# Hybrid decoder step: four scoring steps for eight, the own token through TensorE, copies of the value product on ScalarE

## What is computed

```python
gate = jnp.einsum('bshd,bnhd->bhsn', q, k_mean)        # one number per head and block
_, idx = lax.top_k(gate, ks)                           # the 3 best blocks
s_sel = jnp.einsum('bqhd,bhqnjd->bhqnj', q_c, k_sel) - slopes * dist
s_own = jnp.einsum('bqhd,bjhd->bhqj', q_c, k_own)      # for a sample: its own new token
p = jax.nn.softmax(concat(s_sel, s_own))
o = einsum(p_sel, v_sel) + einsum(p_own, v_own)
```

## Time and profile before

| | |
|---|---|
| median of 3 runs | 666.08 us (663.58 to 670.77) |
| the profiled execution | 667.34 us, its span 665.6 us |
| PE, DVE, ACT, POOL busy | 566.9, 420.4, 240.2, 135.4 us |
| mean granted TensorE clock | 0.922 |
| the eight turns | 121.45 us to 360.42 us |

### The profile page before, as it was taken

How to read it: one execution, slowest core, us unless ns; L and a number is a source line. 1 busy time by engine, 2 the same in 40 slices (tenths; PEclk the granted TensorE clock), 3 DMA queues, 4 the chain that set the end, 5 groups by cost and what they waited for, 6 DMA issues and landing times.

```text
span 665.6 us, 10279 instructions
## 1 busy us (share of the span) xinstructions
PE 566.9 (85%) x4080; PEld 463.0 (70%) x4080; DVE 420.4 (63%) x735; ACT 240.2 (36%) x438; POOL 135.4 (20%) x206
## 2 busy tenths in 40 slices
PE   4869998778778797868679597977999999999997
PEld 2657686546455554536446586966999999999997
DVE  2425793598797979887865366346655666664441
ACT  1102311454462727342135143136433344333341
POOL 8110100274746657661010000000000000000000
PEclk9969998798888887979988899976999999999999
DMA  8998297439896887898472739644775845466600
GB/s 264 384 413 311 73 406 245 160 127 387 285 401 254 348 330 279 342 373 349 162 296 85 261 130 391 225 133 148 232 254 191 286 158 182 120 173 175 176 34 33
DMA packets 85199, 159.30 MB, mean 239 GB/s; under 512 B 2572, under 2 KB 61112, under 8 KB 81047
## 3 DMA queue, kind: packets, MB, share of 16 engines
q1 hardware_dynamic: 79328, 89.27, 40.4%
q0 software_dynamic: 5120, 67.71, 25.7%
q10 hardware_dynamic: 703, 1.67, 0.7%
HBM read 156.39 MB, written 2.72 MB: 239 GB/s over the span
## 4 chain that ended last, share of the span: by engine, by line
PE 61%; DVE 15%; DMA 13%; POOL 4%; ACT 3%; issue 3%; ACTq 1%; SPq 1%; POOLq 0%; DVEq 0%
PE acc L1200 13%; PE acc L1291 12%; PE acc L1292 11%; PE acc L1293 11%; DMA kring<-in_cache_k,rowof 5%; PE chain L1376 4%; DVE prod L819 3%; DVE sall L826 3%; POOL cvT L471 3%; PE acc L1167 3%; DMA wring<-in_w_ada 2%; DMA wring<-in_w_out 2%; DMA wring<-in_w_attn_proj 1%; DMA wring<-in_w_ffn_in 1%; DVE wlo L896 1%
## 5 line engine op out<-in xcount | busy, mean ns | idle before, releaser
L1200 PE MATMUL acc<-hT,wring 128*128 128x264 f32 x576 | 158.8, 430 | 3.7 <-DVE hT L785 1.9
L896 DVE TENSOR_TENSOR wlo<-wring,whi 128x1024 fp32r<-128x1024 f32 (+2 forms) x92 | 101.9, 1108 | 93.2 <-ACT whi L499 92.5
L1200 PEld LDWEIGHTS acc<-hT,wring 128*128 128x128 f32 x576 | 116.5, 210 | 36.7 <-issue 13.5
L1291 PE MATMUL acc<-xlo,whi 128*128 128x264 f32 x416 | 123.9, 298 | 13.5 <-DVE xT L1070 7.4
L499 ACT ACTIVATE whi<-wring 128x1024 fp32r<-128x1024 f32 (+2 forms) x92 | 88.2, 963 | 119.4 <-PE acc L1293 94.3
L1292 PE MATMUL acc<-xhi,wlo 128*128 128x264 f32 x416 | 120.9, 291 | 0.0
L1293 PE MATMUL acc<-xhi,whi 128*128 128x264 f32 x416 | 120.9, 291 | 0.0
L471 POOL TENSOR_TENSOR cvT<-cvT,cprod 128x256 f32<-128x256 f32 x120 | 88.2, 735 | 86.6 <-ACT cprod L499 71.3
L1291 PEld LDWEIGHTS acc<-xlo,whi 128*128 128x128 f32 x416 | 81.2, 195 | 18.2 <-DVE wlo L896 8.6
L819 DVE TENSOR_TENSOR prod<-kring,qbc 128x1024 f32<-128x1024 f32 x64 | 77.4, 1210 | 7.5 <-DMA kring<-in_cache_k,rowof 3.3
L1292 PEld LDWEIGHTS acc<-xhi,wlo 128*128 128x128 f32 x416 | 81.7, 197 | 0.1
(11 more groups left out here) (221 smaller groups left out, 623.5 us busy)
## 6 DMA issues: line engine op xcount, KB each, us to landing
wring<-in_w_ada SPq DMA_DIRECT2D x24, 1024.0 KB, 8.2
wring<-in_w_ffn_in SPq DMA_DIRECT2D x22, 1024.0 KB, 6.8
wring<-in_w_in SPq DMA_DIRECT2D x12, 1024.0 KB, 19.1
wring<-in_w_ffn_out SPq DMA_DIRECT2D x16, 704.0 KB, 5.8
wring<-in_w_out SPq DMA_DIRECT2D x4, 1024.0 KB
wring<-in_w_in SPq DMA_DIRECT2D x6, 512.0 KB, 14.3
wring<-in_w_in SPq DMA_DIRECT2D x4, 768.0 KB, 12.2
wring<-in_w_conv_proj SPq DMA_DIRECT2D x2, 1024.0 KB, 15.7
```

Of the source, the lines that this page charges most:

```text
L896: v.tensor_tensor(wlo[:, place, 0:n, :], w, whi[:, place, 0:n, :].bitcast(F32), ALU.subtract)\
L1200: ins = mm(bank[:, 0:R], w[:, k, P * t:P * t + P], src[:, k, :], start=k == 0, stop=k == KD - 1)
L1291: mm(bank[:, 0:R], whi[:, place, k - k0, :], lo[:, k, :], start=k == 0, stop=False)
```

## The change

- **Four scoring steps**: STEPS is 4, each pair works on 2048 elements a partition. The first multiply of the next sample stands at the turn's start, ahead of the copy of the page sums; the others are moved too.
- **K in three places**: a chunk of K goes in turn to the two halves of `kring` and to place 2 of the weight ring, which the turns' weights give up (they use places 0 and 1). The ring of tap products has four places.
- **PSUM**: the small products of the chain go to a bank of their own, `small`; `chain` holds only the value product, `psO` shares the bank of `psT`. The next L1313 doesn't wait for the last reads of the turn.
- **Own token**: its V row of each sample lies in partitions 32 to 39 (`vrow`), DVE makes an 8 x 8 of probabilities that is zero but for row b (`pown`), and PE adds one more matmul of 8 rows into column group 0 of the value product. DVE's L1016 and L1037 go.
- **Value product**: probabilities `pg` of 8 columns, unpadded; the sums are copied out by ACT; the mask `headof` goes into the sums over partitions, which PE does behind the next prompt scores; ACT copies their result into `oT`.
- **Prompt**: ACT scales the rows of the prompt's probabilities, behind its second batch of tap products; the product with V stands behind the spread of the sums.
- **Ranking of blocks**: one subtraction and two fused operations for four.
- ACT does the convolution's silu (now `conv_rows`) before it copies the last value product.

The core of the diff:

```diff
-STEPS = 8
+STEPS = 4
...
+K_RING = 3
...
+PLACE = dict(zip(SLOTS, [0, 1, 2, 0, 1, 2, 0, 1] + [n % 2 for n in range(B - 1)]))
...
-CONV_RING = 5
+CONV_RING = 4
...
+        psO = psT
...
+        k_place = [kring[:, 0:PC, :], kring[:, PC:PG, :], wring[:, 2, :].rearrange("p (j n) -> p j n", j=PC)]
```

On POOL (gathers), and on ACT in a turn:

```diff
             for b in range(B):
                 add_taps(b, 0)
                 add_taps(b, 1)
-                if b + 2 < B:
-                    gather_k(b + 2, 0)
+                gather_k(CH * b + 5)
                 add_taps(b, 2)
...
-                if b + 2 < B:
-                    gather_k(b + 2, 1)
+                gather_k(CH * b + 6)
...
+                tap_products(b, 1)
+                act.wait_ge(prin_ready, b + 1)
+                for t, (c0, c1) in enumerate(((0, P), (P, 384))):
+                    func(pr[:, c0:c1], pr[:, c0:c1], ACT.Copy, scale=prin[:, t:t + 1]).then_inc(pn_ready, 1)
                 act.wait_ge(pt_ready, b + 1)
                 act.wait_ge(pp_ready, b)
                 func(prT[:, :], psT[:, 0:384], ACT.Copy).then_inc(pc_ready, 1)
-                tap_products(b, 1)
...
+                if b == B - 1:
+                    conv_rows()
+                act.wait_ge(v_used, CH * (b + 1))
+                func(pvm[:, :], pv[:, :], ACT.Copy).then_inc(pvm_ready, 1)
+                if b < B - 1:
+                    gate(FIRST_GATE[b] + 1)
+                act.wait_ge(pv_ready, b + 1)
+                for e in range(2):
+                    rows = slice(DH * e, DH * e + DH)
+                    func(oT[rows, :, S + b], pvT[rows, e:H:2], ACT.Copy).then_inc(o_ready, 1)
```

On PE, the own token and the end of a turn:

```diff
-                        ins = mm(chain[32 * q:32 * q + 32, :], ppad[:, g, :], vring[:, g, :],
-                                 start=g < 4, stop=g >= PG - 4)
+                        ins = mm(pv[32 * q:32 * q + H, :], pg[:, g, :], vring[:, g, :], start=g < 4, stop=PG - 4 < g)
+                        if g == PG - 4:
+                            mm(pv[0:H, :], pown, vrow, start=False, stop=True)
...
-                pe.wait_ge(pvm_ready, b + 1)
-                for t in range(AT):
-                    ins = mm(chain[:, t:t + 1], pvm[:, P * t:P * t + P], ones[:, 0:1], start=True, stop=True)
-                ins.then_inc(pv_ready, 1)
-
                 if b + 1 < B:
                     if b == B - 2:
                         pe.wait_ge(ln_c, 2)
                         sums("lnv", lnsq, CT)
                     prompt_scores(b + 1)
+
+                pe.wait_ge(pvm_ready, b + 1)
+                for t in range(AT):
+                    ins = mm(pvT[:, 2 * t:2 * t + 2], pvm[:, P * t:P * t + P], headof[:, 2 * t:2 * t + 2], start=True, stop=True)
+                ins.then_inc(pv_ready, 1)
                 if b in THIRD:
                     tile(THIRD[b], mix, 2, hT, k1=4)
```

More of the change, by code:

```diff
@@ L476, in _ @@
             pool.wait_ge(w_full[0], 64)
[L477 to L479 removed]
+            gather_k(0)
+            gather_k(1)
+            pool.wait_ge(acc_full, NUMBER[LAST_FILL["k"]] + 1)
+            gather_k(2)
             for c in range(CH):
                 gather_v(0, c)
[L482 removed]
+            gather_k(3)
+            gather_k(4)
             for b in range(B):
@@ L832, in score @@
                 add_up(b, half)
-            for half in range(4):
+            for half in range(STEPS // 2):
                 score(0, half)
@@ L1032, in _ @@
                     dve.wait_ge(stored, 16 * 7)
-                dve.wait_ge(pv_ready, b + 1)
-                dve.wait_ge(dve_step, at_own)
-                for e in range(2):
-                    rows = slice(DH * e, DH * e + DH)
-                    v.tensor_tensor(oT[rows, :, S + b], own[rows, :], chain[rows, 0:AT], ALU.add).then_inc(o_ready, 1)
-                add_up_next(7)
             for t in range(1, KD):
@@ L1263, in _ @@
             to_rows("vn1", vT, P, P)
-            to_rows("vs", vT, S, B)
+            bank = bank_for("vs")
+            for t in range(4):
+                ins = mm(bank[32:32 + B, P * t:P * t + P], vT[:, t, S:R], ident[:, :], start=True, stop=True)
+            ins.then_inc(acc_full, 1)
             w = slot_ready("glu")
```

228 lines of the change are left out of this document (108 added, 120 removed).

## The result

The changed kernel takes 676.75 us (median of 4 runs, 676.53 to 677.72), the kernel before 666.71 in the same comparison: 1.015 times as long, 95% interval 1.0093 to 1.0206. The forecast was 664.8, slightly faster, with 0.24 for slower. The time lies inside the range of 654 to 677 by a hair, but the direction was wrong: a slight gain was forecast, and the kernel is slower, by an interval that lies wholly above 1. The profiled execution took 676.85 us, its span is 675.1, that of before 665.6.

The account below looks back on a forecast made before the run. VectorE's serial list bounds each turn's first half, TensorE the second. Turns 1 to 5 -5.9, turn 0 +0.4, turn 6 +1.3, turn 7 +3.0: -1.2 us from 666.1, rounded 664.8; range 654 to 677.

Parts of the forecast that it names:

- PE turns to them at 12.9, behind its gate tile: First half: TensorE takes up ScalarE's row scalings, done near 12.5 us, at 12.9 us; cover 0.4 us.
- a slow tile only eats the last of them: First half: a tile at low clock only uses up TensorE's last wait, 1.5 to 2.3 us before L1367.
- rival 2: From L1367 on, the clock falls in every second half: 1.35 us more in seven turns, 674.3 to 678; chance 0.18.
- a first half over 16.5 (ScalarE or a fall of clock that reaches the sums): Sign of a wrong forecast: L1313 to L1367 takes over 16.5 us, where about 15.6 was expected.
- First half, 15.55 + 0.14: L1313 to L1367, set by VectorE's serial list: 15.55 us, plus 0.14 mean for the glu product; 15.75 before.
- Second half, 13.65 + 0.35: L1367 to the next L1313, set by TensorE: 13.65 us, plus 0.35 for the clock; 14.76 before.
- rival 3: The drain: tiling changes make the own-token product cost 2.1 us in each turn, 671.6 us; chance 0.10.
- The own token, 1.25: Second half: the added own-token matmul costs 1.25 us a turn, between 0.2 and 2.1.
- No wait before the values: Second half: probabilities ready at 18.5 us, TensorE reaches the values at 19.05, so the 1.27 us wait goes.
- Clock: Second halves: one fall of TensorE to 1.2 GHz in five turns, 0.35 us a turn; ends 0 and 1.7.
- Turn 6: Turn with VectorE's centring: own token 1.25 and the mean's sum added, less half of the score steps; +1.3 us.
- Turn 7, +3.0: Last turn: later values, own token, and ScalarE splitting unit 3 after the turned sums start unit 3 near 370; +3.0 us.

Follow-up runs that it names:

- e9: Changed kernel with eight equal scoring steps: a multiply and a reduce of 1024 elements replace each large operation of 2048; 685.44 us, ratio 1.0316.
- e13: Changed kernel with GpSimd's convolution adds cut to one column instead of 256, all waits kept; 675.96 us, ratio 1.0157.
- e2: Changed kernel with the own-token product left out; 661.93 us, ratio 0.9965.
- e7: Changed kernel with the prompt's value product back ahead of the spread-sum matmul L1368; 677.91 us, ratio 1.0158.
- e3: Changed kernel with the first large reduce of a turn ahead of the page-sum copy, in VectorE's idle time; 673.36 us, ratio 1.0109, two runs.
- e1: Changed kernel with the own-token product 128 rows deep at the same place, so the tiling stays; 672.4 us, ratio 1.004.
- e15: e8 with VectorE's large operations one place earlier and the reciprocal for ScalarE's row scaling behind the third multiply; 651.55 us, ratio 0.9836.
- e8: Changed kernel with own token in turning matmuls, prompt value product before L1368, early first reduce, exponential before transposes copy, turn 7 unit 3 split early; 656.09 us.
- e10: e8 with VectorE shifted as in e15, ScalarE's prompt exponentials before its first products, 14 products before its value-sum copy; 697.64 us, ratio 1.0515.
- e11: e8 with TensorE's transposes of the prompt's probabilities ahead of the second half of the gate tile; 670.95 us, ratio 1.0108.
- e4: Changed kernel where, in turn 7, ScalarE splits unit 3's weights before waiting for the turned sums; 675.79 us, ratio 1.0146, two runs.

## Why the prediction was wrong, point by point

The step that failed in the turns is the first half: "PE turns to them at 12.9, behind its gate tile" and "a slow tile only eats the last of them". TensorE turned to the transposes at 14.2 to 15.1 us, behind a tile at half clock, and ScalarE's exponential behind them became a second path that ended as late as VectorE's list, at 15.4 to 16.7 us for a forecast of 15.2. First halves took 16.63 us for 15.69, which is 4.7 of the 6.2 us that the turns 1 to 5 missed the forecast by; the rest is the own token, 1.88 us for 1.25, less the 0.35 that was put in for the clock. In turn 7 it was the slow clock in the value products, 1.7 us that were not put in, and the size of what ScalarE's order costs, 2.4 us or more for 1.5. The time came out near that of rival 2 (674.3 to 678), but by luck: its mechanism, a fall of the clock in every second half, was in none of them in turns 1 to 5. The forecast's own sign of being wrong, "a first half over 16.5 (ScalarE or a fall of clock that reaches the sums)", is what happened.

- **Large DVE operations at 2.28 us**: right, 2277 and 2278 ns. DVE idle "about 6 us" at the turn's end: right (6.24). Four steps: worth 8.7 us (e9).
- **First half, 15.55 + 0.14**: wrong, 16.63. Two steps failed. VectorE's list was reckoned without GpSimd: where no add runs beside L984, in turn 3, the maxima are ready at 7.85 us as forecast (7.84) and the list ends at 15.44 (forecast 15.2); where one does, L984 alone takes 0.36 us more, and the list ends at 15.8 to 16.7. And "a slow tile only eats the last of them" was wrong: the slow tile delays the transposes and ScalarE's copy, behind which the exponential stands. The changed kernel's trace shows each of the two ending last in some turn, and e13 took the first away and the half stayed. How long the half would be without the slow tile alone is not shown: no run here kept the clock up and left the rest as it is.
- **Second half, 13.65 + 0.35**: the sum is nearly right (14.29), by two errors. The own token, 1.25, was 1.88 to 1.90 (5.45 us against 3.57 before and 3.55 in e2); the 0.35 for the clock was 0 there, since the clock fell in first halves. The own token, put between the middle case and the upper bound's 2.1, is the mis-sized term, and the price of rival 3 was near: two rounds of 0.88, and about 0.1 where 0.3 was put for restarts.
- **No wait before the values**: nearly; 0.35 us in turn 2, and it was the moved prompt product that hid the rest (e7).
- **Clock**: the forecast had one fall in five turns, and in a place where it costs 1.7 us. In turns 1 to 5 there was one fall in every turn, in the first half, where the kernel before had mostly one in each half. In e3 and e1 (turns 1 to 3) and in e15 (turns 1 and 3) second halves are slow as rival 2 has it; in e8, whose first halves are as short as those of e3, none of the five is. What decides the place is not shown.
- **Turn 6**: +2.2 for +1.3; 0.6 of the 0.9 is the own token's price.
- **Turn 7, +3.0**: wrong, +7.4. Value stretch 7.15 us against 3.62: own token 1.88 and the clock 1.7 (5.30 us for 3.60; in e10, e11 and e15, which came there at 2.4 GHz, it is 3.6). The first half and what stands ahead of the value products are 0.85 more. And from the first unit to unit 3 it takes 9.58 us, not 6.60. Of these 3.0 us ScalarE's order is 2.4: with its split ahead of the wait for the turned sums (e4) the stretch is 7.19 us; the other 0.6 lie between units 2 and 3 (3.36 us for 2.80). So the forecast had the right cause for this stretch and half its size (370 less the 361.9 at which its first unit starts is 8.1, 1.5 more than 6.60). What it left out in turn 7 is the slow clock in the value products.
- **K rows, lost weight slot, PSUM bank**: at nothing, right: no wait for K rows in turns 1 to 5 (3.3 us before), and the rest of the program is 0.2 us shorter.

## What to carry to other kernels

A matmul that joins a stream of products running side by side is to be priced in rounds: here, 8 or 128 rows deep, it cost one round where it stood last or left the tiling as it is, and two where it changed the tiling and broke a round. When two engines hand work to each other, follow every path into a hand-over, not the longest alone: here two ended within half a us of each other, and taking one away gave nothing. Read a small edit by the stretch that it touches and not by the whole time: e4 gave 2.4 us there and 1.0 in the median, since other parts vary by more than that. Before an engine takes over a copy from another, see what is queued ahead of it at whose pace: in e10, six more products ahead of a copy meant 3.57 us of wait and a slow turn.

## What the runs showed of the hardware that I had not expected

- Small VectorE operations on SBUF are two to over three times as long when they start while GpSimd adds: L984 (8x8, one input) 0.52 for 0.16 us, L1034 0.70 for 0.22, L1032 up to 0.68 for 0.29; with adds of one column all are short (e13). In the changed kernel L984 and L1034, when long, end 0.01 to 0.03 us after the add that was running beside them. Where VectorE was first, it isn't longer: in turn 1 L1032 starts 0.1 us ahead of an add and takes 0.29 us. The large reduces and multiplies, 2.27 to 2.29 us, don't change. The Trainium skill, "SBUF — State Buffer", Who interferes with whom, describes such a shared pair of ports, and reduces as free of it; these rows agree.
- The granted clock falls behind waits as short as 1.4 us (e3, e15), but not behind each of them: in turn 2 of the kernel before, the tile behind a wait of 1.75 us ran at full speed. In most of turns 1 to 5 of the changed kernel, e3, e8 and e15 it falls once, and ten entries behind it cost 1.7 us more (4.18 and 4.16 for 2.49), whether the turn is 31 us long or 28.
- An 8-row product of 512 columns takes as long by itself (0.95 us) as one of 128 rows does (0.95 in e1).
